# Moving the adaLN products of an attention layer ahead of it, running its latent tokens first, and turning the router's product round

## What is computed

```python
for i in range(2):
    # shift, scale, gate from silu(cond) @ ada_w[i] (1024 x 6144), for both kinds of tokens
    hp, hs = modulate(y_p, norm_mix[i], sh1_p, sc1_p), modulate(y_s, norm_mix[i], sh1_s, sc1_s)
    if i == 0:  mp, ms = conv_module(hp, ...), conv_module(hs, ...)
    else:       # q, k RMS-normed per head; rope on the latent ones; softmax with a sink logit
        mp, kc, vc = attn_context(hp, ...)                     # prompt keys only
        ms = attn_latent(hs, cache_k, cache_v, ...)            # own keys and 128 cached keys
    y_p, y_s = y_p + g1_p * mp, y_s + g1_s * ms
    # moe: scores = sigmoid(x @ router_w); top 8 of 64 within the 4 best of 8 groups
    y_p = y_p + g2_p * moe(modulate(y_p, norm_ffn[i], sh2_p, sc2_p), ...)
    y_s = y_s + g2_s * moe(modulate(y_s, norm_ffn[i], sh2_s, sc2_s), ...)
return y_p, y_s, new_k (kc), new_v (vc)
```

## Time and profile before

| | us |
|---|---|
| device time, median of 3 runs | 1518.48 (1517.93 to 1519.35) |
| device time of the profiled execution | 1518.69 |
| its span, first to last instruction | 1516.9 |
| busy in it: PE, DVE, ACT | 1429.9, 461.3, 294.4 |
| from `moe_done` of layer 0 (757.9) to the first router matmul of layer 1 (946.2) | 188.3 |

### The profile page before, as it was taken

One profiled execution on the slowest core, in us unless ns is written; L12 is line 12 of the kernel. 1 busy time (PEld: TensorE's weight loads), 2 busy tenths in 40 slices (PEclk: granted clock), 3 DMA queues, 4 the chain that ended last, 5 costly groups with the idle time before them and its releaser, 6 DMA issues.

```text
span 1516.9 us, 23827 instructions
## 1 busy us (share of the span) xinstructions
PE 1429.9 (94%) x9544; PEld 851.1 (56%) x9544; DVE 461.3 (30%) x1449; ACT 294.4 (19%) x602; POOL 0.2 (0%) x4
## 2 busy tenths in 40 slices
PE   5798889999999999999888989999999999999997
PEld 2675775565555655556443647855565555555554
DVE  0699261222222222222234322522222222222222
ACT  2301241111111111111122212211111111111111
POOL 0000000000000000000000000000000000000000
PEclk8899889999999999999998569899999999999999
DMA  8989467699999999999744542796999999999990
GB/s 310 374 332 351 162 250 313 245 385 399 403 391 412 386 403 399 409 386 409 291 173 177 218 167 71 292 386 238 410 385 404 402 395 412 393 395 395 410 399 39
DMA packets 80640, 499.45 MB, mean 329 GB/s; under 512 B 10633, under 2 KB 15409, under 8 KB 23760
## 3 DMA queue, kind: packets, MB, share of 16 engines
q1 hardware_dynamic: 80592, 498.79, 82.2%
HBM read 497.45 MB, written 1.31 MB: 329 GB/s over the span
## 4 chain that ended last, share of the span: by engine, by line
PE 91%; DVE 5%; DMA 3%; ACT 1%; issue 1%; SPq 0%; DVEq 0%; ACTq 0%
PE ps L766 31%; PE ps L797 16%; PE ps L747 12%; PE ps L807 9%; PE ps L507 4%; PE ps L550 3%; PE ps L578 3%; PE ps L703 2%; PE ps L482 2%; PE ps L642 1%; PE ps L496 1%; PE ps L616 1%; DMA ring<-in_conv_w_dram 1%; DVE W L1188 1%; DVE hbf L1188 1%; PE ps L688 1%
## 5 line engine op out<-in xcount | busy, mean ns | idle before, releaser
L766 PE MATMUL ps<-ring,W 128*64 128x512 f32 x2048 | 453.3, 595 | 1.1 <-ACT W L1048 1.0
L766 PEld LDWEIGHTS ps<-ring,W 128*64 128x64 f32 x2048 | 166.2, 137 | 282.5 <-issue 277.6
L797 PE MATMUL ps<-ring,W 128*64 128x512 f32 x1024 | 233.9, 599 | 1.0 <-DVE W L1438 1.0
L747 PEld LDWEIGHTS ps<-W,hbf 128*128 128x128 bf16 x3168 | 183.1, 98 | 56.4 <-issue 54.2
L747 PE MATMUL ps<-W,hbf 128*128 128x128 bf16 x3168 | 199.2, 220 | 3.0 <-DVE W L1416 2.2
L1444 DVE TENSOR_TENSOR ypart<-ps,ypart 128x512 fp32r<-128x512 f32 x132 | 91.3, 692 | 191.0 <-ACT ypart L1059 191.0
L807 PE MATMUL ps<-comb,ypart 128*128 128x256 f32 x1056 | 142.5, 287 | 2.8 <-DVE ypart L1444 2.8
L1433 DVE SCALAR_TENSOR_TENSOR W<-W,ps 128x256 f32<-128x256 f32 x66 | 31.7, 480 | 352.1 <-ACT W L1053 352.1
L797 PEld LDWEIGHTS ps<-ring,W 128*64 128x64 f32 x1024 | 67.8, 136 | 117.5 <-issue 109.7
L807 PEld LDWEIGHTS ps<-comb,ypart 128*128 128x128 f32 x1056 | 130.2, 189 | 6.2 <-DVE ypart L1444 4.6
L1048 ACT ACTIVATE W<-ps 128x512 f32<-128x512 f32 x132 | 78.9, 597 | 273.7 <-PE ps L747 273.7
(11 more groups left out here) (196 smaller groups left out, 894.0 us busy)
## 6 DMA issues: line engine op xcount, KB each, us to landing
ring<-in_exp_w_gate_dram SPq DMA_DIRECT2D x128, 1024.0 KB, 8.8
ring<-in_exp_w_up_dram SPq DMA_DIRECT2D x128, 1024.0 KB, 10.8
ring<-in_exp_w_down_dram SPq DMA_DIRECT2D x128, 1024.0 KB, 9.7
S<-in_ada_w_dram SPq DMA_DIRECT2D x48, 1024.0 KB, 7.8
ring<-in_conv_w_dram SPq DMA_DIRECT2D x4, 2048.0 KB, 19.0
S<-in_attn_wqkv_dram SPq DMA_DIRECT2D x1, 6144.0 KB, 25.4
ring<-in_conv_w_dram SPq DMA_DIRECT2D x1, 4096.0 KB, 20.7
S<-in_exp_w_gate_dram SPq DMA_DIRECT2D x4, 1024.0 KB, 11.1
```

What stands on the lines that cost most here:

```text
L747: mm = pe.matmul(PG[:, kk * P:(kk + 1) * P], hbf[:, part, g, 4 * half + kk, :], gbf[:, g, :], start=(n == 0), stop=(n == 2 * 3 - 1))
L766: mm = pe.matmul(PGU[64 * b:64 * b + 64, :].rearrange("p (h f) -> p h f", h=2), xg[:, k, 64 * b:64 * b + 64], gate_up_of(w[b])[:, k], star ...
L797: mm = pe.matmul(bank[64 * b:64 * b + 64, :], hidT[:, j, 64 * b:64 * b + 64], down_of(w[b])[:, j, n * 512:(n + 1) * 512], start=(j == 0), ...
```

## The change

- **Units 32 to 47 move.** Nine of them are loaded at the end of layer 0's experts, into ring slots 0, 1 and 3 as these come free; the other seven follow at the start of layer 1. PE multiplies four of them before the sum of squares of layer 1 and four behind it; their result is turned among the products with `wqkv`. Two more stand behind the first two scores, and one in each of the first six steps.
- **The latent tokens go first**: their products with `wqkv`, their norm, and steps 0 to 3 of the heads (`HEADS`). Buffers move so that the attention uses ring slot 2 alone. In layer 1 experts 0 and 1 are loaded when units 43 and 46 have been used, experts 2 and 3 during the product with `wo`, and the shared expert's weights behind them.
- **The router's product is turned round**: the 64 columns of `rw` are held and 128 tokens stream, each kind of tokens into its own half of the partitions, chunk by chunk for both kinds. ACT copies the logits, PE turns them with one more transpose, and the sigmoid reads that.
- **Tables are called ahead**: `load_table` runs a function on one element, so that its table is loaded there.

```diff
-    return u - EARLY if u < EARLY + 6 else 4 + u % 2
+    v = u - EARLY
+    return 6 + (v if v < 9 else v - 9)
...
+        ada_late = ring_f[:, 0:2 * EW].rearrange("p (s n) -> p s n", s=6)
+        ada_last = ring_f[:, 3 * EW:4 * EW].rearrange("p (s n) -> p s n", s=3)
...
+        HEADS = [(1, j) for j in range(NKV)] + [(0, j) for j in range(NKV)]
...
-                for s in range(2):
-                    load_expert(l, s, s, "gu")
-                for s in range(2):
-                    load_expert(l, s, s, "dn")
                 else:
+                    load_ada(range(EARLY + 9, N_UNITS))
                     sp.wait_ge(at_qkv, 6)
-                    load_ada(range(EARLY, EARLY + 6))
-                    sp.wait_ge(at_nrm, 1)
-                    sp.wait_ge(at_copied, 1)
+                    sp.dma_start(wo, attn_wo[0].rearrange("(k p) n -> p k n", p=P)).then_inc(ld_wo, 16)
+                    sp.wait_ge(at_nrm, 2)
                     sp.dma_start(new_k[0, 0].rearrange("t h d -> t (h d)"),
                                  qkv[:, 0, NH * HD:(NH + NKV) * HD]).then_inc(stored, 16)
                     sp.dma_start(new_v[0, 0].rearrange("t h d -> t (h d)"),
                                  qkv[:, 0, (NH + NKV) * HD:QKVW]).then_inc(stored, 16)
-                    load_ada(range(EARLY + 6, EARLY + 8))
-                    sp.wait_ge(ada_used, EARLY + 4)
-                    sp.dma_start(wo, attn_wo[0].rearrange("(k p) n -> p k n", p=P)).then_inc(ld_wo, 16)
-                    load_ada(range(EARLY + 8, N_UNITS))
+                    for s in range(2):
+
+                        sp.wait_ge(ada_used, EARLY + 12 + 3 * s)
+                        load_expert(l, s, s, "gu")
+                        load_expert(l, s, s, "dn")
+                    sp.wait_ge(pj_out, 5)
+                    sp.wait_ge(ada_used, N_UNITS)
+                    sp.wait_ge(stored, 32)
+                    for s in range(2, 4):
+                        load_expert(l, s, s, "gu")
+                        load_expert(l, s, s, "dn")
                     sp.wait_ge(pj_out, 8)
                     load_shared(1)
-                    sp.wait_ge(stored, 32)
-                for s in range(2, 4):
-                    load_expert(l, s, s, "gu")
-                for s in range(2, 4):
-                    load_expert(l, s, s, "dn")
                 load_extra(l, 1)
                 sp.wait_ge(sh_done, l + 1)
...
-                    sp.wait_ge(pe_dn[0], 6)
+
                     sp.dma_start(wqkv, attn_wqkv[0].rearrange("(k p) n -> p k n", p=P)).then_inc(ld_qkv, 16)
+                    sp.wait_ge(pe_dn[0], 2 * PAIRS)
+                    load_ada(range(EARLY, EARLY + 6))
+                    sp.wait_ge(pe_dn[0], 2 * PAIRS + 2)
+                    load_ada(range(EARLY + 6, EARLY + 9))
...
             for l in range(L):
                 if l == 1:
+
+                    ada_products(range(EARLY, EARLY + 4), ps[2])
                     sum_squares(4, 0)
+                    ada_products(range(EARLY + 4, EARLY + 8), ps[2])
...
                     for n in range(3):
-                        qkv_product(0, n)
-                    qkv_product(1, 0)
-                    qkv_product(1, 1)
+                        qkv_product(1, n)
+                    ada_transposes(4, ps[2])
...
-                    qk_transposes(0, ps[0:3])
-                    qkv_product(1, 2)
+                    pe.wait_ge(mod_ready, 5)
+                    qkv_product(0, 2)
+                    qk_transposes(1, ps[3:6])
...
-                    units = {i: range(36 + i, 37 + i) for i in range(4)}
-                    units |= {5: range(40, 43), 6: range(43, 46), 7: range(46, 48)}
                     pe.wait_ge(y_ready, KC)
                     at_scores(0)
                     at_scores(1)
-                    ada_products(range(EARLY, EARLY + 4), ps[7])
+                    ada_products(range(EARLY + 8, EARLY + 10), ps[7])
                     for i in range(G * NKV):
                         at_transposes(i)
                         if i + 2 < G * NKV:
                             at_scores(i + 2)
-                        if i == 4:
-                            ada_transposes(4, ps[7])
-                        if i == 5:
-                            pe.wait_ge(mod_ready, 5)
-                        ada_products(units.get(i, []), ps[7])
+                        if i < 6:
+                            ada_products([EARLY + 10 + i], ps[7])
                         at_values(i)
...
-                for g in range(G):
-                    for k in range(KC):
+                for k in range(KC):
+                    for g in range(G):
                         pe.wait_ge(h_ready[g], (2 * l + 1) * KC + k + 1)
-                        mm = pe.matmul(ps[7][:, g * NE:(g + 1) * NE], hT[:, k, g * T:(g + 1) * T], rw[:, l, k, :],
+                        mm = pe.matmul(ps[7][64 * g:64 * g + 64, 0:T], rw[:, l, k, :], hT[:, k, g * T:(g + 1) * T],
                                        start=(k == 0), stop=(k == KC - 1))
                 mm.then_inc(rt_logits, 1)
...
+                        if g == h == 0:
+                            pe.wait_ge(rt_rows, l + 1)
+                            pe.transpose(ps[7][:, 2 * P:2 * P + 2 * NE], logits, ident).then_inc(rt_turned, 1)
...
+            def load_table(function):
+
+                act.activation(spare[:, 1:2], spare[:, 0:1], function)
 
             def squares(src, n, ready, value, bank=7):
+                load_table(ACT.Sqrt)
...
+                    load_table(ACT.Sigmoid)
...
+                    load_table(ACT.Silu)
...
+                    ada_copy(4, ps[2])
+                    qkv_copies(1)
+                    qk_roots(1)
                     qkv_copies(0)
-                    qk_roots(0)
...
-                    qkv_copies(1)
+                    load_table(ACT.Exp)
 
                     def exps(i):
...
                                        ACT.Copy).then_inc(at_otc, 1)
 
                 squares(yT, 3 if l == 0 else 5, pj_done, lambda k: KC * l + k + 1)
+                load_table(ACT.Sigmoid)
                 affine(l, 1)
                 act.wait_ge(rt_logits, l + 1)
-                act.activation(scores[:, :, :].rearrange("p g e -> p (g e)"), ps[7][:, 0:2 * NE], ACT.Sigmoid
-                               ).then_inc(rt_score, 1)
+                act.activation(logits, ps[7][:, 0:T], ACT.Copy).then_inc(rt_rows, 1)
+                act.wait_ge(rt_turned, l + 1)
...
                 else:
 
                     nqk = NH + NKV
-                    for g in range(G):
-                        dve.wait_ge(at_copied, g + 1)
+                    ada_finish(4, ps[2])
+                    for g in (1, 0):
+                        dve.wait_ge(at_copied, 2 - g)
+                        if g == 0:
+                            dve.wait_ge(at_nrm, 1)
                         v = qkv[:, g, 0:nqk * HD]
                         v3 = v.rearrange("p (h d) -> p h d", d=HD)
```

93 lines of the change are left out of this document (58 added, 35 removed).

## The result

| | before | after |
|---|---|---|
| device time, median | 1518.2 (1517.45 to 1519.35, 4 runs) | 1503.2 (1498.3 to 1503.9, 4 runs) |
| device time of the profiled execution | 1518.69 | 1503.94 |
| its span | 1516.9 | 1502.1 |

The ratio of the times is 0.989, 95% interval 0.987 to 0.992: faster by 15 us. The forecast was 46 us less, and the result lies 6 us above the top of the range.

The account below looks back on a forecast made before the run. The prediction took PE as the bound, at 1.2 GHz in the heads. From 1518.69 us, +2 (start), -4.4 (up to T0), -40.3 (steps), -5 (router) and +1.5 (tables) gave -46.2, so 1472.5, range 1465 to 1497.

Parts of the forecast that it names:

- What bounds the kernel: Whole kernel: PE is 91% of the chain, DMA 3%; in the heads PE is busy 46.8 of 48 us at 1.2 GHz.
- The eight steps: Heads, from the transposes of step 0 to the output's transposes: 81.6 us before, 41.3 forecast, mostly at 2.4 GHz, -40.3.
- the slow end: The eight steps of the heads if all stays at 1.2 GHz: 64.5 us, a saving of 17.1.
- the fast one: The eight steps at 2.4 GHz: 36.3 us, or 41.3 with 3 for a slow stretch and 2 for the last two steps.
- the steps stay at 1.2 GHz: Rival for the heads' steps: saving 17.1 us in place of 40.3, kernel at 1495.7; chance 0.17.
- Up to T0: First product with `wqkv` to the transposes of step 0 (T0): 55.4 us for 59.8, set by DVE, -4.4.
- Start of the products: From `moe_done` to the first product with `wqkv`: +2 us, ends +1 and +5.5, with the unit loads as the risk.
- the risks that were named: Start of layer 1: the eighth unit landing late, start 5.5 us late (rival at 1476), or the first experts waiting for loads.
- Behind the heads: From the output's transposes to the router: only the product with `wo` and a norm, which stay; no change forecast.
- the thin last two steps: Last two of the eight steps, without units: may drop the clock into the product with `wo`, 2 us added.
- The router: Router's product turned, 4.4 us for 7.84 on PE: -2.5 for each layer, -5 for both, ends -6.4 and 0.
- The tables: Second norm of layer 0: load 1.28 and call 0.2 delay all squares, +1.5 us; other calls nothing either way.

Follow-up runs that it names:

- e2: Changed kernel with DVE computing the first maxima in the middle of the prompt's norm instead of behind it: 1468.77 us.
- e1: Changed kernel with nine products that nobody reads in PE's wait ahead of the transposes of step 0: 1471.05 us.
- e6: Kernel before with only the router's product turned, and eight products of two columns at PE's start: 1515.79 us.
- e4: Kernel before with one product of two columns more at PE's start, hidden in a wait: 1521.63 us.
- e8: Changed kernel with 18 products that nobody reads behind the transposes of step 0: 1479.28 us.
- e11: Kernel before, nothing of the change in it, with 18 products that nobody reads behind the transposes of step 0: 1505.15 us.
- e5: e2 with seven of the nine unit loads behind the marker product of layer 0 instead of ahead of it: 1471.48 us.
- e7: e2 without the call of Sqrt ahead of the squares, and with nine products of two columns at PE's start: 1468.77 us.
- e9: e2 with nine products of two columns at PE's start, all calls of tables kept: 1470.08 us.
- e12: e2 with none of the calls of tables (Sqrt, Sigmoid, Silu, Exp), the turned router kept: 1471.09 us.

## Why the prediction was wrong, step by step

**What bounds the kernel**: right, in that PE's clock in the heads is what the change is about. Of the 31 us that are missing, 25 are there.

**The eight steps** (-40.3 forecast, -15.6 measured) is the step that failed. Both ends came out near what was measured: the slow end 64.5 against 65.95, and the fast one 36.3 to 41.3 against the 39.1 and 40.0 of e2 and e1. In part that is luck. "Four of each" counts eight units and four latent scores, but two units and the first two latent scores stand ahead of T0: 1.8 and 3.7 us too much at the fast end (and a prompt step is 3.2, not 3.3). Against it, no waits were counted, and e2 has 4.7 us of them in the steps. At the slow end the scores are 3.4 us too much, against 2.2 us more of waits and rows of before that had run fast (values at 906.61 in 2.00 us for 3.68). The choice between them was wrong. It was argued that "two units and then eight transposes behind the first scores" would make good a fall of the clock. But the wait that the same text had computed ("idle for some 3 us") lies between those units and those transposes, and units and transposes there don't form a dense row. The text said that a fall behind them "is not" made good, and that is the case that came. A wait of 4.18 us is also longer than the 3.82 us behind which the earlier trace rows already show a slow unit. So the trace of before spoke for the rival "the steps stay at 1.2 GHz" (1496, chance 0.17), and 0.6 for the forecast was too much. What came in its place: the wait dropped the clock (T0 in 1.97 us and scores in 3.78, at 0.50), and nothing in the steps brought it back in 66 us, while with the wait filled or taken away they took 40.0 and 39.1. The right question would have been what could close that wait, which is e2.

**Up to T0** (-4.4, measured -6.5): the mechanism was right, DVE's norm ahead of `maxima(0)`; it ran 2 us sooner than worked out. From the first product to DVE's norm behind the last copy were 42.8 us, not 44.9: the 0.453 us for each product came from a row that began at a granted clock of 0.79 (before, 768 to 776), and after has 1.00 from 773 to 815.

**Start of the products** (+2, measured +5.9 with the wait ahead of the marker). The eighth unit was not late, and the first experts did not wait, so the risks that were named did not come. What came was in no term: 2.2 us more at the marker, and four units for the most part at 1.2 GHz behind it, 6.22 us for 3.64. The line "DMA idles ahead of 757.9" held for before only (0.02 from 752 to 756, and 1.02 in after): it was the change that filled DMA there, and the fetch behind the branch paid for that.

**Behind the heads** ("which stay", measured +2.8): the output's transposes 3.68 for 1.97, four small ones 1.06 for 0.60, the product 28.45 for 27.79. The 2 us for "the thin last two steps" were of this kind; even in e1 and e2, where the steps are fast, the output's transposes take 3.68 us behind waits of 1.86 and 0.78.

**The router** (-2.5 each, measured -4.0 and -3.8). The rows of e6 give 2.8 and 2.9 for the turning, as forecast within 0.4, though its median total is only 2.8 us below before for both layers. The other 0.9 to 1.1 is the Sigmoid call, which the prediction put at nothing: it asked what the call hides in the old code, and not where the load would stand in the new.

**The tables** (+1.5): the delay was right to 0.1; the clock it can cost was not seen.

**The end of the kernel** (nothing forecast, measured +3.9): the second wait, between the marker's two records, 3.27 us, and a first one longer by 0.4. No row of before could have told it, e4 can.

**Sum of the misses** (measured less forecast): steps 24.7, the end 3.9, start and marker 3.9, behind the heads 2.8, layer 0 ahead of its experts 1.0, against -2.1 up to T0, -1.3 at the router of layer 1 and -1.4 in the two loops: 31.5, and 46.2 - 14.8 = 31.4. The high end of the range took in the slow steps and nothing for waits outside all terms, so it was short by 6 us. The forecast number, 1472.5, is near what the change gives with the wait ahead of T0 filled (1471.05), but by other terms: e1 also lacks the second wait at the end and has the fast sum of squares, 6 us in all.

## What to carry to other kernels

On a kernel whose chain is TensorE, list every wait of some us that a change leaves or makes, and ask of each at which clock the rows behind it will run, and whether the trace shows work like theirs bringing it back (here scores, units and values in turn did not in 66 us). Close such a wait by moving another engine's work (e2), or else fill it with products that nobody reads (e1: nine of them took 26 us off the steps). And when two parts of a change touch the same path, price each with the other in place.

## What was not expected of the hardware

- Dummy work pays on TensorE: nine products of 128 x 128 by 256 in a wait of 4.18 us took 26 us off the 66 behind it. The clock also comes back within 18 of them (8.55 us in e8 and 10.48 in e11, 7.7 at full speed).
- A taken branch over some 700 PE instructions (an estimate, see e5) cost 1.2 to 1.7 us with DMA idle and 3.9 to 4.4 with DMA at 1.02 of its share (e5 against e2). Each such wait ends 1.24 to 1.59 us behind the landing of a 16 KB packet of the instruction queue; among the kernel's own loads the packet starts about 2 to 3 us later.
- One hidden product at the start made the kernel 2.5 us slower: it moved the code so that a second fetch fell between the marker's two records, 2.7 to 3.3 us in the six traces that have it. Nine products at the start removed it (e7, e9).
- The same wait of 2.75 us was followed by a sum at 3.72 us in three executions, at 5.12 in two and at 6.76 in one; the changed kernel's runs lie 1498.3 to 1503.9. How short a wait must be to be safe in each execution is open: behind 1.08 us the rows were fast (e2), behind 2.75 us not always, behind 1.77 us once slow (e12, 5.41 us for 3.72) and behind 1.76 twice fast (e6). In the last two steps, behind waits of 1.86 and then 0.78 us with little work between, they were slow in e1 and e2 alike.
